# Shifted weights' buffers: four start offsets within 512 bytes, xT behind them, two masks as a spread column

## What is computed

```python
# block 1: nsa_mixer (sparse attention), conv_ffn; block 2: ssd_mixer (chunked scan), conv_ffn
hn = rms_norm(h, gains[0])
m = nsa_mixer(hn, ...)            # or ssd_mixer(hn, ...)
h = h + rms_norm(m, gains[1])
f = conv_ffn(rms_norm(h, gains[2]), ffn_w_up[i], ffn_conv_w[i], ffn_conv_b[i], ffn_w_down[i])
h = h + rms_norm(f, gains[3])

def conv_ffn(h, w_up, conv_w, conv_b, w_down):
    u = causal_dwconv(h @ w_up, conv_w, conv_b)
    val, gate = u[..., :FFN_HIDDEN], u[..., FFN_HIDDEN:]      # FFN_HIDDEN = 2816
    return (jax.nn.silu(gate) * val) @ w_down

# block 3: gdn_branch (gated delta rule), memory_attention over 256 rows, then swiglu
y = jnp.concatenate([y_mix, y_mem], axis=-1) @ w_out[layer]
h = h + rms_norm_2(y, norm_post_mix[layer])
f = swiglu(rms_norm_2(h, norm_pre_ffn[layer]), w_ffn_in[layer], w_ffn_out[layer])
h = h + rms_norm_2(f, norm_post_ffn[layer])
```

## Time and profile before

| | |
|---|---|
| median of 3 runs | 1198.83 us (1198.19 to 1201.48) |
| the profiled execution, its own time | 1202.38 us |
| its span, first to last instruction | 1200.6 us |
| TensorE, matmuls | 1174.5 us busy, 98%, 9852 records |
| TensorE, weight loads | 1078.0 us, 90% |
| VectorE | 847.7 us, 71% |
| ScalarE | 652.0 us, 54% |
| GpSimd | 151.1 us, 13% |
| HBM | 193 MB read, 162 GB/s over the span |
| mean granted TensorE clock | 0.999 |

### The profile page before, as it was taken

The page is one execution under the profiler, slowest core; times in us unless marked ns, Lnnn a source line. Parts: engine busy times, 40 slices in busy tenths (PEclk is TensorE's granted clock), DMA queues, the critical chain, the costliest instruction groups (busy, mean ns, idle before and its releaser), DMA issues.

```text
span 1200.6 us, 23183 instructions
## 1 busy us (share of the span) xinstructions
PE 1174.5 (98%) x9852; PEld 1078.0 (90%) x9852; DVE 847.7 (71%) x1299; ACT 652.0 (54%) x1171; POOL 151.1 (13%) x143
## 2 busy tenths in 40 slices
PE   8999999999999999999999999999999999999998
PEld 8897789999889898878999988999989878999986
DVE  6678777888557988886788865857577776655542
ACT  4657556666446665744666643665434534645431
POOL 1320000000002332100000000103443401000000
PEclk9999999999999999999999999999999999999999
DMA  8832235565634453352755564452231322755540
GB/s 308 269 141 89 100 104 206 189 210 195 231 106 176 155 183 137 115 184 106 281 180 195 188 233 170 170 185 106 104 110 72 111 94 97 281 186 197 181 174 35
DMA packets 31622, 196.67 MB, mean 164 GB/s; under 512 B 4000, under 2 KB 5664, under 8 KB 9376
## 3 DMA queue, kind: packets, MB, share of 16 engines
q1 hardware_dynamic: 27504, 185.17, 43.6%
q10 hardware_dynamic: 4016, 10.03, 2.6%
HBM read 193.09 MB, written 1.05 MB: 162 GB/s over the span
## 4 chain that ended last, share of the span: by engine, by line
PE 88%; DVE 5%; ACT 3%; issue 2%; POOL 1%; DMA 0%; DVEq 0%; POOLq 0%; ACTq 0%
PE bank L539 24%; PE bank L540 24%; PE bank L541 24%; DVE wlo L528 2%; PE bank L1895 1%; PE bank L1133 1%; PE bank L1190 1%; PE bank L1217 1%; ACT whi L520 1%; PE bank L726 1%; PE bank L2539 1%; PE bank L2482 1%; PE bank L3006 1%; POOL rr L668 0%; PE bank L2497 0%
## 5 line engine op out<-in xcount | busy, mean ns | idle before, releaser
L528 DVE TENSOR_TENSOR wlo<-raw,whi 128x1024 fp32r<-128x1024 f32 x322 | 389.1, 1245 | 88.8 <-ACT whi L520 88.1
L539 PE MATMUL bank<-xT,wlo 128*128 128x256 f32 x1488 | 419.0, 282 | 4.3 <-DVE wlo L528 2.1
L541 PE MATMUL bank<-xT,whi 128*128 128x256 f32 x1488 | 413.7, 278 | 0.0
L540 PE MATMUL bank<-xT,whi 128*128 128x256 f32 x1488 | 413.4, 278 | 0.0
L520 ACT ACTIVATE whi<-raw 128x1024 fp32r<-128x1024 f32 (+1 forms) x349 | 349.3, 1048 | 116.4 <-PE bank L541 89.9
L539 PEld LDWEIGHTS bank<-xT,wlo 128*128 128x128 f32 x1488 | 279.1, 188 | 7.9 <-DVE xc L1602 2.8
L540 PEld LDWEIGHTS bank<-xT,whi 128*128 128x128 f32 x1488 | 279.4, 188 | 0.6 <-issue 0.5
L541 PEld LDWEIGHTS bank<-xT,whi 128*128 128x128 f32 x1488 | 279.3, 188 | 0.0
L668 POOL TENSOR_TENSOR rr<-rr,nhalf 128x1 f32<-128x1 f32 x34 | 24.8, 730 | 710.0 <-DVE rr L656 518.9
L539 PE MATMUL bank<-whi,gT 128*128 128x512 f32 x264 | 103.8, 393 | 0.0
L540 PE MATMUL bank<-wlo,gT 128*128 128x512 f32 x264 | 103.7, 393 | 0.0
(11 more groups left out here) (390 smaller groups left out, 1763.7 us busy)
## 6 DMA issues: line engine op xcount, KB each, us to landing
raw<-in_wall SPq DMA_DIRECT2D x173, 1024.0 KB, 4.9
grow<-in_rows ACTq DMA_DIRECT2D x13, 512.0 KB, 5.3
h<-in_x SPq DMA_DIRECT2D x4, 256.0 KB, 5.2
dsk<-in_rows ACTq DMA_DIRECT2D x4, 256.0 KB, 3.1
memx<-in_mem ACTq DMA_DIRECT2D x1, 1024.0 KB, 10.0
out<-h SPq DMA_DIRECT2D x4, 256.0 KB, 2.0
masks<-in_masks SPq DMA_DIRECT2D x1, 580.0 KB, 13.3
D<-Tx ACTq DMA_DIRECT2D x4, 128.0 KB, 6.0
```

What stands on the lines that cost most here:

```text
L528: e.tensor_tensor(low, src, high, SUB).then_inc(*up("dve.low", p))
L539: e.matmul(out, a[1], b[0], start=start, stop=False)
L540: e.matmul(out, a[0], b[1], start=False, stop=False)
L541: return e.matmul(out, a[0], b[0], start=False, stop=stop)
```

## The change

The four buffers of whi become slices of one tile whose stride is 2080 columns (8320 bytes, 16 x 512 + 128), and so do those of wlo. Five small tiles and xT follow directly behind them; h, the scratch tiles, grow, cols, masks, negb and identb come after. The two constant masks are left out of `masks` (128 KB less to load): `half[0]` is column 384 of it, the first of `blk64`, read with step 0 as 128 columns, and `half[1]` column 511, the last of `blk64`. The later masks move up by 256 columns. Nothing else is changed: no instruction, wait or order.

```diff
--- before.py
+++ after.py
@@ -98,7 +98,7 @@
     _ROWS[_n] = (_o, _w)
     _o += _w
 _NROW = _o
-_MASKS = 6 * 128 + 8 * 64 + 8
+_MASKS = 4 * 128 + 8 * 64 + 8
 
 
 def _host_masks():
@@ -106,7 +106,7 @@
     a = np.arange(128)
     r, c = a[:, None], a[None, :]
     same = (r // 64) == (c // 64)
-    m = [r == c, r <= c, (r <= c) & same, same, (r < 64) & (c >= 0), (r >= 64) & (c >= 0)]
+    m = [r == c, r <= c, (r <= c) & same, same]
     m = [x.astype(np.float32) for x in m]
 
     r, c = r % 64, np.arange(64)[None, :]
@@ -306,31 +306,31 @@
 
         banks = [root.enter_context(nc.psum_tensor(f"bank{i}", [128, 512], f32)) for i in range(8)]
         raw = [sb([128, 2048], name="raw") for _ in range(NRAW)]
-        whi = [sb([128, 2048], f32r, name="whi") for _ in range(NHL)]
-        wlo = [sb([128, 2048], f32r, name="wlo") for _ in range(NHL)]
+        whi, wlo = ([w[:, 2080 * i:2080 * i + 2048] for i in range(NHL)]
+                    for w in (sb([128, 2080 * NHL], f32r, name=n) for n in ("whi", "wlo")))
+        valid = sb([128, 2], name="valid")
+        srow = sb([128, 32 + 32 + 16], name="srow")
+        nhalf = sb([128, 1], name="nhalf")
+        ss = sb([128, 8], name="ss")
+        rr = sb([128, 4], name="rr")
+        xT = [sb([128, 8, 256], f32r, name="xT") for _ in range(2)]
+        h = sb([128, 2, 1024], name="h")
+        sqj = sb([128, 1024], name="sqj")
+        xs = sb([128, 1024], name="xs")
+        grow = sb([128, 1024], name="grow")
+        grow2 = sb([128, 1024], name="grow2")
         cols = sb([128, _NCOL], name="cols")
         masks = sb([128, _MASKS], name="masks")
         negf_w = 2 * 128 + 64 + 30 + 8 + 4 + 1
         negb = sb([128, negf_w - 1], bf16, name="negb")
         identb = sb([128, 128], bf16, name="identb")
-        valid = sb([128, 2], name="valid")
-        srow = sb([128, 32 + 32 + 16], name="srow")
-        grow = sb([128, 1024], name="grow")
-        nhalf = sb([128, 1], name="nhalf")
-        h = sb([128, 2, 1024], name="h")
-        xT = [sb([128, 8, 256], f32r, name="xT") for _ in range(2)]
-        ss = sb([128, 8], name="ss")
-        rr = sb([128, 4], name="rr")
-        sqj = sb([128, 1024], name="sqj")
-        xs = sb([128, 1024], name="xs")
-        grow2 = sb([128, 1024], name="grow2")
         sb([128, 16], name="space")
         gains = (grow, grow2)
         ident, tri, tri64, blk64 = (masks[:, 128 * i:128 * i + 128] for i in range(4))
-        half = [masks[:, 512:640], masks[:, 640:768]]
-        level, (idc, tric) = ([masks[:, 768 + 64 * i:832 + 64 * i] for i in v] for v in (range(6), range(6, 8)))
+        half = [masks[:, c:c + 1].to_broadcast([128, 128]) for c in (384, 511)]
+        level, (idc, tric) = ([masks[:, 512 + 64 * i:576 + 64 * i] for i in v] for v in (range(6), range(6, 8)))
         ones1 = masks[:, 255:256]
-        own8 = masks[0:120, 1280:1288]
+        own8 = masks[0:120, 1024:1032]
         neg_qk, neg_sl, neg_gd = negb[:, 0:128], negb[:, 128:256], negb[:, 256:320]
         quad, fourth = negb[0:96, 350:358], negb[0:96, 358:362]
```

## The result

The changed kernel takes **1202.24 us** (median of 10 runs, 1201.64 to 1204.52), the kernel before 1198.4 us (10 runs, 1197.87 to 1202.6) on the same chip: ratio 1.0024, 95% interval 1.0012 to 1.0035. It is slower by 3.8 us; 1193.4 was forecast.

What follows compares the result with a forecast made beforehand. TensorE's matmuls at lines 539 to 541 were taken as the bound (chain 88% on TensorE). Terms -8.0 + 2.3 + 0.3 = -5.4 us, from the median 1198.83: 1193.4 us, range 1186 to 1203, the forecast's own 1187 to 1196.

Steps and rivals of the forecast that it cites:

- (a): 256-column matmuls, xT moving: new gaps (stationary minus moving start, modulo 512 bytes) break the slow rhythm; -8.0 us, ends 0 and -11.2.
- R1: Rival, no change: every distance keeps a slow rhythm and entry decides by chance, half the groups slow; 1199.7 us, chance 0.25.
- (a), second up-projection: First chunk on buffer 0 (gap 64) breaks the slow rhythm, later chunks keep the fast one: -4.2 us, in full.
- the sign that was asked for: Line 540 with xT moving at 276 ns throughout the second up-projection, its 271 groups taking 92.1 us instead of 95.7.
- (a), other stages: Chunks mostly enter separately: buffer 1 stays slow, buffer 2 decays in part, buffers 0 and 3 fast; -3.8 us.
- 826.82 us: Timeline point before the change: xT turns from stationary to moving, gap 320 to 192, and the pitch stays 113.3 ns.
- (b): 512-column down-projections, weights moving, activation stationary: a quarter goes to gap 320, half loss at unseen gaps; +2.3 us, ends -1.3 and +3.8.
- the cycle that was to be looked for: 512-column pitches differing from chunk to chunk in a cycle of four, 233 on buffer 1.
- (c): Each new buffer shifts the gap under a running stream: some 60 shifts x 5 ns, +0.3 us; upper end +1.3.
- (d): Spread masks as stationary operand at lines 1685, 1686, 2228, and smaller masks transfer: nothing taken; ends +2.3 and -0.4 us.
- R2: Rival, slower: up-projection streams lose the fast rhythm at the first load from each next buffer; 1211 us, chance 0.17.
- (e): h, xs, sqj, masks, cols move by less than a stage: nothing charged, ends inside those of (b).

Runs made afterwards that it cites:

- experiment 5: Kernel before with only the weights' buffers' 8320-byte stride and the smaller masks, order of tiles unchanged: 1203.77 us, ratio 0.9992; also holds a table of chunk boundaries over 14 profiles.
- experiment 7: Experiment 2's kernel with gaps 64 and 448, now 0 for gT, yT, yG: 1196.08 us; fourth buffer moved 256 bytes 1199.1, 128 bytes 1198.79; two pads 1200.39.
- experiment 1: Kernel before, unedited, profiled again: 1198.36 us, second up-projection at 276 ns.
- the fast profile: Second profile of the unchanged kernel before, 1198.36 us, with 4.0 us less span than the profile shown earlier.
- experiment 2: Changed kernel without rotation, one gap for all buffers (xT moving/gT, yT, yG): 64/448 1198.19 us, 0/0 1221.86, 128/128 1222.21, 192/448 1209.67, 64/64 1203.29.

## Why the prediction was wrong

**The base: the first step that failed.** "The profiled execution took 1202.38 us ... -5.4 gives 1197.0. The median of the runs is 1198.83, so 1193.4." A difference made against one execution was taken off a median of another kind. The gap between the two, 3.5 us, was in the text, and it is nearly the 4.2 of term (a). In the kind of the median that term is zero. The rival R1, "half the groups slow instead of all", was also priced from the one profile.

**(a), second up-projection.** Right in part: streams are broken at a change of gap (experiments 5 and 7), and the size against the profile shown was right (-4.2). But the sign that was asked for, 276 ns throughout, proves nothing, since the unchanged kernel shows it too (experiment 1). And the reason given was wrong. What turns fast within five matmuls at gap 64 is the beginning of a stretch, and not always. A slow stream under way does not decay there: it stays slow, whole up-projections long. It ends where the gap goes from 192 to 64 (modulo 256) in the middle of the stream, in 14 cases of 22.

**(a), other stages: the second step.** Forecast -3.8; measured, with the losses, +1.0 against the fast profile, of which the moving operand in the mixers gave -1.4. Stretches with xT moving that stay slow are 42 of 113 in the changed kernel, 51 in the fast profile of before, 71 in the one shown. By gap 64, 192, 320 and 448 they are 4 of 26, 18 of 33, 8 of 27 and 12 of 27; so buffer 1 is the worst and buffer 0 the best, as forecast, but each entry is a draw. And a term was missing: the 256-column matmuls with xT stationary. Their gap went from 320, where 10 of 34 stretches are slow, to 64, 192, 320 and 448, where 24 of 34 are; the row of line 540 with xT stationary has its median at 279 ns, and in the fast profile of before at 277. 14 stretches more of about 24 matmuls at 4.4 ns are 1.5 us; the starts gave 1.7 (experiment 1). The prediction counted only xT moving; for these it took 826.82 us, a change of use with xT going over to moving, as a sign that boundaries do no harm. So the forecast missed the median by 8.8 us in two steps of about one size: 4.2 us by the base, and 4.8 in these stages (+1.0 for -3.8). That 1202.24 lies within 1186 to 1203 is owed to the room made for R1; the forecast's own range ended at 1196.

**(b), 512 columns.** +2.3 forecast, 2.2 measured. For the unseen gaps "half the loss" was taken: 64 costs all of it (233.3) and 192 none (228.9), so the half was right as a mean. One cycle of the changed kernel's second down-projection, first matmul of each chunk at gap 320, 192 and 64:

```profile
699.21 0.39 PE L539 MATMUL bank<-whi,gT 128*128 128x512 f32 x1
...
704.79 0.39 PE L539 MATMUL bank<-whi,gT 128*128 128x512 f32 x1
...
710.29 0.39 PE L539 MATMUL bank<-whi,gT 128*128 128x512 f32 x1
```

5.58 and 5.50 us over 24 are 232.5 and 229.2 ns: the cycle that was to be looked for, though its period is two buffers, not four. The distance counts modulo 256, not 512.

**(c), (d).** With xT moving no fast stream was lost at a boundary, as forecast. R2 came true where it was not placed, with xT stationary, at 1.7 us. Of R1 the mechanism, an entry that is in part a draw, came nearest to what the runs showed. The spread masks take no longer to load.

**(e), the order.** "Nothing is charged" was an error of its own, which the rotation hid. Order and masks without the rotation gave +11 us (experiment 2, gap 192). The text bounded the moved tiles by (b), as if only operands of the dense matmuls could matter.

**The rule.** The Trainium skill ("SBUF — State Buffer", "Who interferes with whom") has TensorE read moving operand and weights by two independent ports and wait on no one. Here the pitch of one and the same matmul goes with the distance of the two operands: 226.7, 229.2, 232.1 and 233.3 ns. By that rule "no change" would have been the forecast. It would have been closer to the mark, but for the wrong reason.

So the change does two things. At before's gaps its order catches nearly every up-projection; with the rotation, streams that begin slow are freed within a few matmuls or at the second boundary. What is left is a kernel with almost no spread at 1202, where before has 1198.5 most of the time on some chips and 1202 to 1211 on others: of before's 115 runs on five chips 69 are of the lowest kind, 31 some 4 us and 15 some 8 us or more above it, and on two of the chips only 4 of 34 are of the lowest. Whether the changed kernel would win on those two was not measured.

## What to carry to other kernels

Ahead of a sum, lay the profiled execution's own time beside the median: if they differ by about one of the sum's terms, find the kind of run that each is, and charge that term to the right one. Where a stream has two stable pitches, a layout is judged by the times of ten or more runs in their kinds; a change anywhere, even in a tile that the stream does not read, can move the odds by more than its own cost. For float32r matmuls the distance of stationary and moving operand is worth setting: with 512 columns a multiple of 256 bytes was best (226.7 ns), with 256 columns that was the worst (120.0), and 64 bytes from it let the fast pitch (113.3) exist.

## What the runs showed of the hardware

- The pitch of a 128x128 by 512 float32r matmul goes with the gap modulo 256 bytes, at a granted clock of 0.997 to 1.000: 0 gives 226.7 ns, 192 gives 228.9, 128 about 232.1, 64 gives 233.3. (Gaps 64 and 320 agree, as do 192 and 448; one stretch at 448 ran at 233.4.)
- At 256 columns gaps 0 and 128 have one pitch each, 120.0 and 118.7 ns. The gaps between have two, 113.3 and 117.8, and a stream keeps the one that it is in over nine hundred matmuls.
- Past its fifth matmul only a changed gap or a pause changed the pitch of a stream (table in experiment 5). Why one direction frees and the other loses, and why 8 of 22 were not freed, stays open.
- After a pause or another matmul a stretch of 256 columns was fast in 322 of 542 cases at gap 64 (modulo 256) and in 65 of 529 at gap 192. What else ahead of a stream bears on its pitch stays open.
- How often a stream is caught differs from chip to chip with the same program: before's median was 1198.5, 1198.7, 1198.9, 1202.7 and 1204.3 us on five.
